# An attention's bias added by TensorE in PSUM, and its powers and sums taken by ScalarE head by head

## What is computed

```python
# NSA, a block of 128 queries; 8 heads in 2 groups of 4, head width 64
s_c = einsum('bghqd,bgnd->bghqn', qb, k_cmp) + head_bias(dist_c)   # compressed blocks
s_s = einsum('bghqd,bgqkd->bghqk', qb, k_sel) + bias_s             # selected keys
s_w = einsum('bghqd,bgkd->bghqk', qb, k_w) + bias_w                # window
o = g0 * softmax(s_c) @ v_cmp + g1 * softmax(s_s) @ v_sel + g2 * softmax(s_w) @ v_w
# attention over the memory: 4 heads of width 256, no bias
p = softmax(einsum('bqhd,bmhd->bhqm', q, k))
o = einsum('bhqm,bmhd->bqhd', p, v)
```

## Time and profile before

| | |
|---|---|
| three runs | 2703.3, 2707.64, 2711.72 us; median 2707.64 |
| the profiled execution | 2702.18 us |
| its span, first to last instruction | 2700.4 us |
| mean granted PE clock | 0.952 |
| busy share PE, DVE, ACT, POOL | 91%, 66%, 43%, 28% |
| chain of waits, share of the span | PE 74%, DVE 19%, ACT 3% |
| NSA attention | about 167 to 295 us |
| attention over the memory | 362.8 to 393 us |

### The profile page before, as it was taken

The page is one execution under the profiler, slowest core; times in us unless marked ns, Lnnn a source line. Parts: engine busy times, 40 slices in busy tenths (PEclk is TensorE's granted clock), DMA queues, the critical chain, the costliest instruction groups (busy, mean ns, idle before and its releaser), DMA issues.

```text
span 2700.4 us, 38709 instructions
## 1 busy us (share of the span) xinstructions
PE 2456.6 (91%) x15906; PEld 2212.8 (82%) x15906; DVE 1792.4 (66%) x2734; ACT 1163.0 (43%) x1894; POOL 767.6 (28%) x366
## 2 busy tenths in 40 slices
PE   6968788999999999997878978789999999999997
PEld 5856678999999888885767966589999999888885
DVE  4575455987888555555587275365997888655555
ACT  3333234444444444443543254234444444444443
POOL 3000102896666100001000043101896666100000
PEclk8878889999999999999989988899999999999999
DMA  5412224555444566664422433235555454566663
GB/s 165 133 48 77 86 87 141 165 171 149 148 144 146 176 188 189 187 187 133 125 94 86 133 114 113 63 104 174 168 171 151 148 148 146 171 190 187 188 188 109
DMA packets 108566, 384.37 MB, mean 142 GB/s; under 512 B 13007, under 2 KB 16000, under 8 KB 107816
## 3 DMA queue, kind: packets, MB, share of 16 engines
q1 hardware_dynamic: 108392, 381.91, 47.0%
HBM read 380.79 MB, written 1.06 MB: 141 GB/s over the span
## 4 chain that ended last, share of the span: by engine, by line
PE 74%; DVE 19%; ACT 3%; issue 1%; POOL 1%; DMA 1%; SPq 0%; DVEq 0%; POOLq 0%; ACTq 0%
PE psum L370 20%; PE psum L371 20%; PE psum L372 20%; PE psum L1795 4%; PE psum L402 2%; DVE peer_experts L1703 1%; DVE peer_experts L1702 1%; PE psum L2415 1%; DVE peer_experts L1679 1%; DVE peer_experts L1671 1%; DVE peer_experts L1673 1%; PE psum L549 1%; PE psum L2185 1%; DVE peer_experts L1676 1%; DVE peer_experts L1668 1%
## 5 line engine op out<-in xcount | busy, mean ns | idle before, releaser
L370 PE MATMUL psum<-acts_high,weight_parts 128*128 128x256 f32 x3152 | 931.2, 295 | 70.6 <-DVE acts_low L581 28.4
L371 PE MATMUL psum<-acts_low,weight_parts 128*128 128x256 f32 x3152 | 902.3, 286 | 0.0
L372 PE MATMUL psum<-acts_high,weight_parts 128*128 128x256 f32 x3152 | 901.4, 286 | 0.0
L349 POOL TENSOR_TENSOR weight_parts<-weight_ring,weight_parts 128x1024 fp32r<-128x1024 f32 x276 | 695.8, 2529 | 646.4 <-ACT weight_parts L338 645.8
L338 ACT ACTIVATE weight_parts<-weight_ring 128x1024 fp32r<-128x1024 f32 x681 | 714.7, 1050 | 182.3 <-PE psum L372 100.4
L343 DVE TENSOR_TENSOR weight_parts<-weight_ring,weight_parts 128x1024 fp32r<-128x1024 f32 x405 | 498.1, 1231 | 358.3 <-ACT weight_parts L338 358.3
L370 PEld LDWEIGHTS psum<-acts_high,weight_parts 128*128 128x128 f32 x3152 | 614.3, 195 | 88.6 <-issue 42.7
L371 PEld LDWEIGHTS psum<-acts_low,weight_parts 128*128 128x128 f32 x3152 | 616.3, 196 | 2.7 <-issue 1.7
L372 PEld LDWEIGHTS psum<-acts_high,weight_parts 128*128 128x128 f32 x3152 | 615.0, 195 | 0.0
L370 PE MATMUL psum<-weight_parts,peer_coef 128*128 128x512 f32 x1024 | 405.2, 396 | 4.0 <-issue 3.9
L372 PE MATMUL psum<-weight_parts,peer_coef 128*128 128x512 f32 x1024 | 405.0, 395 | 0.0
(11 more groups left out here) (384 smaller groups left out, 2504.9 us busy)
## 6 DMA issues: line engine op xcount, KB each, us to landing
weight_ring<-in_peer_down SPq DMA_DIRECT2D x128, 512.0 KB, 3.6
weight_ring<-in_peer_up SPq DMA_DIRECT2D x128, 512.0 KB, 4.3
weight_ring<-in_peer_u SPq DMA_DIRECT2D x128, 512.0 KB, 3.6
weight_ring<-in_peer_v SPq DMA_DIRECT2D x128, 512.0 KB, 4.2
weight_ring<-in_w_in SPq DMA_DIRECT2D x88, 512.0 KB, 3.7
weight_ring<-in_w_out SPq DMA_DIRECT2D x16, 512.0 KB, 3.5
weight_ring<-in_peer_w_q SPq DMA_DIRECT2D x16, 512.0 KB, 3.5
weight_ring<-in_w_in_v SPq DMA_DIRECT2D x10, 512.0 KB, 4.0
```

The source lines that it names most:

```text
L349: q.e.tensor_tensor(self.low, self.ring, self.high.bitcast(F32), ALU.subtract).then_inc(*self.unit.ready.once())
L370: q.e.matmul(out, sh, mh, start=first, stop=False)
L371: q.e.matmul(out, sh, ml, start=False, stop=False)
L372: return q.e.matmul(out, sl, mh, start=False, stop=last)
```

## The change

In the steps with a group, PE adds the bias: after each head's scores it multiplies the identity with the head's bias table into the same bank (`stop=False`, then `start=False`). PE now waits for the bias tables. DVE takes the maximum straight from PSUM and negates it (4 numbers per query) instead of subtracting it from the whole area. ACT takes the powers head by head from PSUM, with the negated maximum as bias, and accumulates each head's sum into `z`, so DVE's sum is gone. The steps over compressed blocks stay as they were, but for the marks. In the attention over the memory the same is done with two heads, with no bias to add.

```diff
@@ Attend.tensor
             keys = s.kv[("ks", "kw")[self.branch]]
+            q.wait_ge(*s.bias_came)
             for h in range(HPG):
-                last = q.e.matmul(c.bank(b0, 2)[:, n * h:n * (h + 1)], s.q[rows, h, q_i], keys[rows, T - n:T],
-                                  start=True, stop=True)
+                out = c.bank(b0, 2)[:, n * h:n * (h + 1)]
+                q.e.matmul(out, s.q[rows, h, q_i], keys[rows, T - n:T], start=True, stop=False)
+                last = q.e.matmul(out, c.ident[:, :], s.bias[i][:, HPG * self.g + h, :], start=False, stop=True)
@@ Attend.vector
         else:
-            last = q.e.tensor_tensor(self.area, c.bank(b0, 2)[:, 0:HPG * n].rearrange("p (h n) -> p h n", h=HPG),
-                                     s.bias[i][:, HPG * self.g:HPG * (self.g + 1), :], ALU.add)
-        last.then_inc(*self.biased.once())
-        q.wait_ge(self.biased)
-        settle(c, q, "vector", q.e.tensor_reduce(self.mx, self.area, AX, ALU.max))
-        q.e.tensor_tensor(self.area, self.area, over(self.mx, n, 2), ALU.subtract).then_inc(*self.shifted.once())
+            settle(c, q, "vector", q.e.tensor_reduce(self.mx, self.scores, AX, ALU.max))
+            q.e.tensor_scalar(self.mx, self.mx, -1.0, None, ALU.mult).then_inc(*self.shifted.once())
         yield
         yield
         q.wait_ge(self.powers)
-        settle(c, q, "vector", q.e.tensor_reduce(self.z, self.area, AX, ALU.add))
+        if self.g is None:
+            settle(c, q, "vector", q.e.tensor_reduce(self.z, self.area, AX, ALU.add))
         settle(c, q, "vector", q.e.reciprocal(self.z, self.z))
@@ Attend.scalar
         q.wait_ge(self.shifted)
-        q.e.activation(self.area, self.area, ACT.Exp).then_inc(*self.powers.once())
+        if self.g is None:
+            last = q.e.activation(self.area, self.area, ACT.Exp)
+        else:
+            for h in range(HPG):
+                last = q.e.activation(self.area[:, h, :], self.scores[:, h, :], ACT.Exp, bias=self.mx[:, h:h + 1],
+                                      accum_out=self.z[:, h:h + 1])
+        last.then_inc(*self.powers.once())
@@ AttendMemory.vector
         settle(c, q, "vector", q.e.tensor_reduce(self.mx, src, AX, ALU.max))
-        q.e.tensor_tensor(self.area, src, over(self.mx, T, 2), ALU.subtract).then_inc(*self.shifted.once())
+        q.e.tensor_scalar(self.mx, self.mx, -1.0, None, ALU.mult).then_inc(*self.shifted.once())
         yield
         yield
         q.wait_ge(self.powers)
-        settle(c, q, "vector", q.e.tensor_reduce(self.z, self.area, AX, ALU.add))
         q.e.reciprocal(self.z, self.z).then_inc(*self.total.once())
@@ AttendMemory.scalar
-        q.e.activation(self.area, self.area, ACT.Exp).then_inc(*self.powers.once())
+        for y in range(2):
+            last = q.e.activation(self.area[:, y, :], self.c.bank(self.b)[:, T * y:T * y + T], ACT.Exp,
+                                  bias=self.mx[:, y:y + 1], accum_out=self.z[:, y:y + 1])
+        last.then_inc(*self.powers.once())
```

More of the change, by code:

```diff
@@ L1146, in __init__ @@
         self.bank_free = c.bank_free[self.b0] + c.bank_free[self.b0 + 1]
-        self.scored, self.biased, self.shifted = c.mark("attn_scored"), c.mark("nsa_biased"), c.mark("attn_shifted")
+        self.scores = c.bank(self.b0, 2)[:, 0:HPG * self.n].rearrange("p (h n) -> p h n", h=HPG)
+        self.scored, self.shifted = c.mark("attn_scored"), c.mark("attn_shifted")
         self.powers, self.total, self.weighed = c.mark("attn_powers"), c.mark("attn_total"), c.mark("attn_weighed")
@@ L1176, in tensor @@
         yield
-        q.wait_ge(self.weighed, self.biased)
+        q.wait_ge(self.weighed)
         if self.g is None:
@@ L1198, in vector @@
                     "p (h n) -> p h n", h=HPG), steps, ALU.add)
-        else:
-            last = q.e.tensor_tensor(self.area, c.bank(b0, 2)[:, 0:HPG * n].rearrange("p (h n) -> p h n", h=HPG),
-                                     s.bias[i][:, HPG * self.g:HPG * (self.g + 1), :], ALU.add)
-        last.then_inc(*self.biased.once())
-        q.wait_ge(self.biased)
-        settle(c, q, "vector", q.e.tensor_reduce(self.mx, self.area, AX, ALU.max))
-        q.e.tensor_tensor(self.area, self.area, over(self.mx, n, 2), ALU.subtract).then_inc(*self.shifted.once())
+            settle(c, q, "vector", last)
+            settle(c, q, "vector", q.e.tensor_reduce(self.mx, self.area, AX, ALU.max))
+            q.e.tensor_tensor(self.area, self.area, over(self.mx, n, 2), ALU.subtract).then_inc(*self.shifted.once())
+        else:
+            settle(c, q, "vector", q.e.tensor_reduce(self.mx, self.scores, AX, ALU.max))
+            q.e.tensor_scalar(self.mx, self.mx, -1.0, None, ALU.mult).then_inc(*self.shifted.once())
         yield
```

## The result

| | before | changed |
|---|---|---|
| median | 2709.79 us | 2717.76 us |
| lowest to highest | 2703.3 to 2712.83 (20 runs) | 2709.21 to 2722.99 (20 runs) |
| profiled execution | 2702.18 us | 2718.4 us |
| values of the memory attention begin | 384.19 us | 391.98 us |

The ratio of the changed kernel to the one before is 1.003, with a 95% interval of 1.0024 to 1.0037. The forecast was a little faster, 2704 with a range of 2694 to 2711; the kernel became 8 us slower and lies outside it.

The account below looks back on a forecast made before the run. PE, busy 2456.6 of 2700.4 us, bounds the kernel, so only stages where it stands still can gain. NSA -0.35 and the memory attention -3.2, together -3.6, gave 2698.6 profiled, 2704 as median; range 2694 to 2711.

Parts of the forecast that it names:

- the memory attention: Attention over the memory: three chains' tails and transposes 2.3 us earlier, the fourth chain 0.9 us shorter; sum -3.2 us.
- the price of PE's products: Identity products adding the bias in NSA: 0.26 and 0.45 us per head, 1.05 and 1.8 per step, 11.5 in all.
- C and D: NSA's second pair of Attend steps, 128 columns a head: scores 2.6 us later, tails shorter, stage +1.6 us.
- A and B: NSA's first pair of steps, the first over blocks: identity products run at the half clock, stage +0.3 us.
- E and F: NSA's third pair of steps, the second over blocks: PE +1.05, ACT +1.0, DVE -0.7, stage +1.3 us.
- G: NSA's lone middle step, 256 columns a head: PE is full, so its added products count whole, +1.8 us.
- H and I: NSA's last pair of steps, 256 columns a head: transposes 3.2 us earlier, products behind 1.35 shorter; stage -4.55 us.
- J: NSA's lone last step beside the output products: scores +1.8 us, DVE and ACT's path -2.6; stage -0.8 us.
- ACT per head: Exponential with its sum read, in steps with a group: 0.38 us at 128 columns, 0.48 at 256.
- ACT becomes the bound: Slower rival, chance 0.2: exponentials of some 24 heads on the path cost 0.25 us more each, +6, so 2710 us.
- The order behind the projection's keep: On ACT in NSA's second pair of steps, a keep stands ahead of the exponentials; later PE moves both, +3.1 us.
- the clock holds: Faster rival, chance 0.2: PE's pauses shrink, the clock stays up through NSA's outputs and memory attention, -8.2, so 2696 us.

Follow-up runs that it names:

- grouped: The changed kernel with all identity products of a step first, then its scores, the bank cleared by the first product alone; 2699.56 us, ratio 0.9962.
- crossed: The changed kernel with scores and identity products still alternating, but never writing the same columns twice in a row; 2718.6 us.
- half twice: The changed kernel with each identity product replaced by a second copy of the head's score product, for timing only; 2697.09 us.
- DVE adds: The changed kernel, but in NSA DVE adds the bias into SBUF and takes the maximum there; 2697.62 us, ratio 0.9956; run again, 2699.74 us.
- full height: The changed kernel in its order, but score products over all 128 partitions, both groups summed, for timing only; 2698.68 us.

## Why the prediction was wrong

**The step that failed** is the price of PE's products, "0.26 and 0.45 us per head, 1.05 and 1.8 us per step at the full clock, 11.5 us in all". It came from the earlier trace rows, rows in which products of one height follow each other. In the changed order nearly every one of the 64 products changes between 64 and 128 partitions and costs 0.195 us more than a product among its like. Against the forecast's figures that is 0.16 us on 32 products and some 0.15 on the other 32, about 10 us of PE's time. In C and D the scores were to take 2.6 us more and took 5.0 more. The prediction did look at the mix of heights, but only for what it takes away (scores of two groups running beside each other, 1.0 and 0.5 us). With a change at every fourth product, as in the grouped version, the stages come near the forecast or better: A and B +0.5 (forecast +0.3), C and D +0.6 (+1.6), E and F -0.3 (+1.3), G +1.8 (+1.8), H and I -4.9 (-4.55), J -1.7 (-0.8), outputs -1.4 (0); NSA -5.3 in all, and the memory attention -5.4 (-3.2). So the other terms were on the cautious side: with PE's order put right the kernel takes 2699.56 us, less than the forecast 2704.

**A second term was missing**: the clock falling while PE is busy. The prediction watched only pauses. It cost about 2.4 us of E and F's +5.9 (a projection of 8.4 us for 6.0). In the three profiles with strict alternation of heights (the changed kernel's two and crossed) it took 8.0 to 8.4 us. In those of the others it took about 6, except 7.5 in half twice (half speed from 208.5 on) and 7.2 in the first profile of DVE adds, neither of which alternates heights. That the alternation causes the fall is therefore not shown.

**What held.** ACT per head: 0.343 and 0.45 us against 0.38 and 0.48; it was no loss, so the rival "ACT becomes the bound" is out, and the powers and sums on ACT are the useful part of the change in NSA. The Trainium skill, "ScalarE: Activation LUTs", section "What ACT_TABLE_LOAD costs", gives 0.29 and 0.40 without the sum (an estimate from its figures). The trace has 0.05 more at both widths, with a read of the sum for which that page of the Trainium skill gives no price. The order behind the projection's keep came as described: whatever PE loses moves C's and D's exponentials. In H and I the first pause went and the second is 0.79 us (forecast about 1), and in J it is 2.38 (forecast 2.4); in the memory attention 1.78 (forecast 1.9). PE's timeline after:

```profile
274.95 1.09 PE L1188 MATMUL psum<-ident,nsa_s 128*128 128x128 f32 x8 [0.79 <-DVE nsa_s L1217]
289.00 1.09 PE L1188 MATMUL psum<-ident,nsa_s 128*128 128x128 f32 x8 [2.38 <-DVE nsa_s L1217]
...
381.71 2.72 PE L1531 MATMUL psum<-ident,xa_s 128*128 128x128 f32 x12 [1.78 <-DVE xa_s L1547]
...
390.18 1.11 PE L1531 MATMUL psum<-ident,xa_s 128*128 128x128 f32 x4 [2.96 <-DVE xa_s L1547]
```

H and I gained 2.3 us for 4.55 because their sixteen products take 10.1 us for the 7.6 forecast. J's transposes ran at full clock, but the outputs behind them still at a mean of 0.68, 15.5 us: the rival "the clock holds" did not occur there. It occurred in part in full height and DVE adds again, whose outputs took 12.9 us at a mean of 0.84. The memory attention's -3.9 answers to -3.2. That the median lies above the profiled execution was said, but not how far the profile of before is at the fast end: 2702.2 against a median of 2709.8 in twenty runs.

**The side.** A slower result had a chance of 0.07, on the ground of ACT and of "what I overlook". PE's price was taken as known because rows gave one, and no bound was set above it. Nowhere in the trace of before do 64 and 128 partitions take turns product by product, but heights do take turns in the outputs, where two records of 15 partitions (line 1257) stand between eight of 128 (line 1260). PE's timeline before, at full clock:

```profile
289.53 0.43 PE L1257 MATMUL psum<-nsa_pt_cmp,v_cmp 15*64 15x128 f32 x2
289.89 1.09 PE L1260 MATMUL psum<-nsa_pt,nsa_vt 128*64 128x128 f32 x8
290.90 0.43 PE L1257 MATMUL psum<-nsa_pt_cmp,v_cmp 15*64 15x128 f32 x2
```

From the second of the eight records on, the starts are 0.109 us apart, so ten such records would take 1.09 us; they take 1.37, from 289.53 to 290.90. That is 0.14 us for each of the two changes, about one load of these weights (0.13 to 0.14 us). A bound of one load per product could have been read there.

## What to carry to other kernels

Where fp32 products of 64 and of 128 partitions meet on TensorE, put those of one height together: each change cost about 0.195 us here, as much as a load of weights. For a bias added through the identity that is one order of two loops, worth 18 us here (2717.76 against 2699.56); clear the bank with the first product only. Even so the bias on PE gained nothing over the add on DVE (2697.62): what paid was ACT's share, powers with the sum in the same call. A price read from rows holds for the neighbours that those rows have: when a change puts two kinds of product beside each other that never were, bound the price upwards by a load that doesn't overlap.

## What was not expected of the hardware

- The change of height: 0.417 us per product of 128 columns, 0.222 without; 0.627 and 0.43 at 256. It doesn't matter which columns are written (crossed: 0.417).
- The granted clock fell to half in the midst of products (at 188.8 in the second profile of the changed kernel, at 216 in both), 1.6 to 4.1 us after pauses of only 0.96 and 1.42 us. What the chip weighs there stays open.
- ACT reads an accumulated sum in a record of its own of 0.19 to 0.25 us, 0.09 of it ahead of the next call. Heads of 128 columns come 0.343 us apart out of PSUM and 0.385 out of SBUF (DVE adds).
- The stretch between the first and the second PEER's selection took between 1423.5 and 1430.5 us over fourteen traces that don't differ there, and the values of the changed kernel began at 391.98 in one profile and at 395.91 in the other. One profile each is too little for a change of 8 us; the medians of twenty runs tell it.
